# Expert stage of a two-block network: two-part gather and scatter matmuls, six weight slots, interleaved pairs of experts

## The reference

```python
def hier_moe(h, w_rg, b_rg, w_re, b_re, w_eg, w_eu, w_ed):
    ...                                  # router: 2 of 32 experts for each token
    for e in range(N_EXPERTS):           # 32
        hid = jax.nn.silu(t @ w_eg[e]) * (t @ w_eu[e])       # 1024 -> 512
        out = out + gates[:, e:e + 1] * (hid @ w_ed[e])      # 512 -> 1024
    return out.reshape(bsz, s, d)
```

## Time and profile before

| | us |
|---|---|
| median of 3 runs | 2285.81 |
| fastest and slowest run | 2283.96, 2295.26 |
| span of the profiled execution | 2275.8 |

### The profile page before, as it was taken

The page is one execution under the profiler, slowest core; times in us unless marked ns, Lnnn a source line. Parts: engine busy times, 40 slices in busy tenths (PEclk is TensorE's granted clock), DMA queues, the critical chain, the costliest instruction groups (busy, mean ns, idle before and its releaser), DMA issues.

```text
span 2275.8 us, 29449 instructions
## 1 busy us (share of the span) xinstructions
PE 1985.1 (87%) x11980; PEld 1551.8 (68%) x11980; DVE 871.2 (38%) x1464; ACT 735.0 (32%) x1018; POOL 119.3 (5%) x112
## 2 busy tenths in 40 slices
PE   7967798888898777999988879987799998797997
PEld 5844443334443377778887879877787888797986
DVE  3052121111221232533355756533343335575653
ACT  1230011111111132557345434322255634533432
POOL 0000000000000000320210000000031030000000
PEclk9987899999999975999999989998599999998999
DMA  5403588988988732223223334543123322342452
GB/s 208 178 1 157 233 352 337 379 368 360 375 361 359 321 139 107 75 98 126 78 109 148 130 114 180 202 168 141 75 75 111 112 111 101 123 148 112 186 192 102
DMA packets 30887, 412.36 MB, mean 181 GB/s; under 512 B 3600, under 2 KB 5040, under 8 KB 5808
## 3 DMA queue, kind: packets, MB, share of 16 engines
q1 hardware_dynamic: 30768, 410.68, 46.0%
HBM read 408.84 MB, written 1.84 MB: 180 GB/s over the span
## 4 chain that ended last, share of the span: by engine, by line
issue 86%; PE 6%; POOL 5%; DVE 1%; DMA 1%; ACT 0%; SPq 0%; POOLq 0%; DVEq 0%; ACTq 0%
POOL work_mem L1650 5%; PE bank L703 3%; PE bank L711 2%; DMA work_mem<-in_const 1%; PE bank L798 0%; PE bank L735 0%; PE bank L780 0%; POOL small L1658 0%; PE bank L737 0%; PE bank L738 0%; DVE ht_mem L1689 0%; PE bank L773 0%; DVE work_mem L1809 0%; POOL small L1631 0%; DVE work_mem L1826 0%
## 5 line engine op out<-in xcount | busy, mean ns | idle before, releaser
L926 PE MATMUL bank<-wring,gates_mem 128*64 128x512 f32 x1024 | 238.5, 623 | 47.3 <-DMA wring<-in_w 40.7
L2012 DVE TENSOR_TENSOR w_lo<-wring,w_hi 128x2048 fp32r<-128x2048 f32 x88 | 201.3, 2292 | 188.2 <-ACT w_hi L1445 188.2
L1445 ACT ACTIVATE w_hi<-wring 128x2048 fp32r<-128x2048 f32 x88 | 168.5, 1915 | 303.4 <-PE bank L1002 171.8
L1001 PE MATMUL bank<-mixed_hi,w_hi_early 128*128 128x256 f32 x960 | 243.7, 291 | 6.8 <-DVE mixed_lo L2020 4.2
L1445 ACT ACTIVATE w_hi_early<-wring 128x2048 fp32r<-128x2048 f32 x80 | 152.9, 1912 | 265.3 <-PE bank L1002 176.1
L1002 PE MATMUL bank<-mixed_lo,w_hi_early 128*128 128x256 f32 x960 | 238.3, 285 | 0.0
L2012 DVE TENSOR_TENSOR w_lo<-wring,w_hi_early 128x2048 fp32r<-128x2048 f32 x80 | 183.2, 2290 | 124.7 <-ACT w_hi_early L1445 124.7
L926 PEld LDWEIGHTS bank<-wring,gates_mem 128*64 128x64 f32 x1024 | 88.4, 143 | 192.3 <-issue 192.3
L1006 PE MATMUL bank<-mixed_hi,w_lo 128*128 128x256 f32 x1472 | 208.8, 285 | 0.0
L1001 PEld LDWEIGHTS bank<-mixed_hi,w_hi_early 128*128 128x128 f32 x960 | 186.3, 194 | 12.3 <-issue 6.1
L1006 PEld LDWEIGHTS bank<-mixed_hi,w_lo 128*128 128x128 f32 x1472 | 192.2, 194 | 0.0
(11 more groups left out here) (404 smaller groups left out, 3216.2 us busy)
## 6 DMA issues: line engine op xcount, KB each, us to landing
wring<-in_w SPq DMA_DIRECT2D x192, 2048.0 KB, 8.4
cst<-in_const SPq DMA_DIRECT2D x1, 1273.0 KB, 7.6
prm<-in_prm SPq DMA_DIRECT2D x3, 381.0 KB, 8.5
x_mem<-in_x SPq DMA_DIRECT2D x1, 1024.0 KB, 4.9
out_x<-x_mem SPq DMA_DIRECT2D x1, 1024.0 KB, 3.9
rel_skew<-work_mem SPq DMA_DIRECT2D x1, 768.0 KB, 3.5
work_mem<-in_prm SPq DMA_DIRECT2D x1, 512.0 KB, 12.3
work_mem<-rel_skew SPq DMA_DIRECT2D x1, 512.0 KB, 3.6
```

The source lines that it names most:

```text
L926: mm = pe.matmul(out[half, :], x_e[:, pair, k, half], w[e][:, k, :], start=(k == 0), stop=(k == KT - 1))
L1001: pe.matmul(out, w[0][:, k, cols], x[0][:, k, :], start=(k == 0), stop=False)
L1445: act.activation(hi, w, ACT.Copy).then_inc(hi_ready, 1)
L2012: dve.tensor_tensor(lo, w, hi, ALU.subtract).then_inc(lo_ready, 1)
```

## The change

- **Gather.** The normed rows `xn` are split once into `xn_hi` (ACT) and `xn_lo` (DVE), both fp32r. `pick` is done once a turn for both pairs: for each of eight column tiles and two token tiles, `xn_hi` and `xn_lo` are the weights, and all 256 columns of `one_hot` move. Four banks instead of two and two. ACT, not DVE, writes `x_e`, times the gain.
- **Scatter.** `turn` now transposes the bare 0/1 matrix, and two small matmuls give each place its gate weight (`slot_gate`). The output of `down` is scaled by it and split into `ye_hi` (ACT) and `ye_lo` (DVE); `spread` sums both pairs and both parts in PSUM: 16 fp32r matmuls a turn in four banks, and DVE adds to `x` four times a turn, not eight.
- **Order.** pick, both turns, gate 0, up 0, gate 1, flip 0, up 1, down_a 0, flip 1, down_b 0, down_a 1, down_b 1, spread.
- **Slots.** Six: the four of `wring`, `work_mem[:, 0:4096]` and `yt_mem`. The chunks are loaded in the new order of use. The first six are issued in the first block, each as its slot comes free, with semaphores of their own.
- `slots` of the next turn is made after `up 0`.

```diff
-MOE_STEPS = [("pick", 0), ("turn", 0), ("gate", 0), ("up", 0), ("pick", 1), ("flip", 0), ("turn", 1), ("down", 0),
-             ("gate", 1), ("up", 1), ("spread", 0), ("flip", 1), ("down", 1), ("spread", 1)]
-MOE_JOBS = {"pick": 2, "down": 2, "spread": 4}
+MOE_STEPS = [("pick", 0), ("turn", 0), ("turn", 1), ("gate", 0), ("up", 0), ("gate", 1), ("flip", 0), ("up", 1),
+             ("down_a", 0), ("flip", 1), ("down_b", 0), ("down_a", 1), ("down_b", 1),
+             ("spread_a", 0), ("spread_b", 0)]
+MOE_JOBS = {"pick": 4, "spread_a": 2, "spread_b": 2}
+MOE_SLOTS = 6
+MOE_CHUNKS = [(w, pair, e) for w, pair in (("gate", 0), ("up", 0), ("gate", 1), ("up", 1), ("down", 0), ("down", 1))
+              for e in range(2)]
...
-    x_e, hid_b, hid_t = view(gates_mem, 0, PAIRS, KT, P), view(gates_mem, 2048, PAIRS, 512), view(gates_mem, 3072, PAIRS, 4, P)
-    y_b, spread_w = view(gates_mem, 4096, PAIRS, D), view(gates_mem, 6144, PAIRS, S)
-    one_hot, weighted = (view(gates_mem, at, TT, 2 * PAIRS, CAP) for at in (6656, 7168))
+    x_e, hid_b, hid_t = view(gates_mem, 0, KT, PAIRS, P), view(gates_mem, 2048, PAIRS, 512), view(gates_mem, 3072, PAIRS, 4, P)
+    ye_hi = view(parts("ye_hi", "gates_mem", 4096, PAIRS * D), 0, PAIRS, D)
+    ye_lo = view(parts("ye_lo", "ht_mem", 0, PAIRS * D), 0, PAIRS, D)
+    spread_w = view(parts("spread_w", "gates_mem", 6144, PAIRS * S), 0, PAIRS, S)
+    one_hot = view(parts("one_hot", "gates_mem", 6656, 2 * TT * PAIRS * CAP), 0, TT, 2 * PAIRS, CAP)
+    one_hot_f, weighted = (view(gates_mem, at, TT, 2 * PAIRS, CAP) for at in (6656, 7168))
+    xn_hi = view(parts("xn_hi", "work_mem", 4096, TT * D), 0, TT, D)
+    xn_lo = view(parts("xn_lo", "xn_mem", 0, TT * D), 0, TT, D)
...
+            return slot(s)
+        return work_mem[:, 0:CHUNK_COLS] if s == SLOTS else yt_mem
...
+        def expert_chunk(c, turn):
+            sp.dma_start(moe_slot(c), d["w1"][PRE_CHUNKS + chunk_from[c] + turn * turn_chunks]).then_inc(
...
+        for c, j in ((0, pre["kd"][1]), (1, pre["vd"][1]), (4, pre["pv"][1]), (2, pre["out"][1]), (3, pre["out"][3]),
...
             sp.wait_ge(bank_full[j.bank], j.count())
-        sp.wait_ge(rel_loaded, 16)
...
-        for j in pre["ydt"]:
-            sp.wait_ge(bank_read[j.bank], j.count())
-        sp.dma_start(gain_row, d["gain"][0]).then_inc(gain_loaded, 16)
-        with sp.Fori(0, MOE_TURNS) as turn:
-            for c in range(turn_chunks):
-                j = moe[chunk_users[c - SLOTS]][-1]
-                sp.wait_ge(bank_full[j.bank], j.count(turn - 1 if c < SLOTS else turn))
-                sp.dma_start(slot(c), d["w1"][PRE_CHUNKS + c + turn * turn_chunks]).then_inc(w_landed[c % SLOTS], 16)
-        for c in range(turn_chunks - SLOTS, turn_chunks):
+            expert_chunk(c, 0)
+            if c == 4:
+                for j in pre["ydt"]:
+                    sp.wait_ge(bank_read[j.bank], j.count())
+                sp.dma_start(gain_row, d["gain"][0]).then_inc(gain_loaded, 16)
+        with sp.Fori(0, MOE_TURNS - 1) as turn:
+            for c in range(MOE_SLOTS, turn_chunks + MOE_SLOTS):
+                j = moe[chunk_users[c - MOE_SLOTS]][-1]
+                sp.wait_ge(bank_full[j.bank], j.count(turn))
+                if c < turn_chunks:
+                    expert_chunk(c, turn)
+                else:
+                    expert_chunk(c - turn_chunks, turn + 1)
+        for c in range(MOE_SLOTS, turn_chunks):
+            j = moe[chunk_users[c - MOE_SLOTS]][-1]
+            sp.wait_ge(bank_full[j.bank], j.count(MOE_TURNS - 1))
...
-                        for k in range(4):
+                        for k in range(2):
+                            cols = slice((2 * n + k) * P, (2 * n + k + 1) * P)
                             for i in range(TT):
-                                mm = pe.matmul(psum[j.bank][:, k * P:(k + 1) * P], xn[:, i, (4 * n + k) * P:(4 * n + k + 1) * P],
-                                               one_hot[:, i, two, :], start=(i == 0), stop=(i == TT - 1))
-                        if n == 0:
...
+                                pe.matmul(psum[j.bank][:, k * S:(k + 1) * S], xn_hi[:, i, cols], one_hot[:, i],
+                                          start=(i == 0), stop=False)
+                                mm = pe.matmul(psum[j.bank][:, k * S:(k + 1) * S], xn_lo[:, i, cols], one_hot[:, i],
+                                               start=False, stop=(i == TT - 1))
+                        mm.then_inc(r.bank_full[j.bank], 1)
...
-                        mm = pe.transpose(out[:, i * P:(i + 1) * P], weighted[:, i, two, :], ident)
+                        pe.transpose(out[:, i * P:(i + 1) * P], one_hot_f[:, i, two, :], ident)
+                    for i in range(TT):
+                        mm = pe.matmul(out[:, S:S + 1], weighted[:, i, two, :], C("one"), start=(i == 0), stop=(i == TT - 1))
+                    mm.then_inc(r.bank_full[j.bank], 1)
...
+                        if step == "gate" and pair == 0 and k % 2 == 0:
+                            copied(r["pick", 0][k // 2])
...
+                elif step in ("down_a", "down_b"):
+                    n = ("down_a", "down_b").index(step)
+                    if n == 0:
+                        copied(r["flip", pair][0])
+                    w = weights("down", pair)
+                    ready(j)
+                    for ft in range(4):
+                        for e in range(2):
+                            half = slice(e * CAP, (e + 1) * CAP)
+                            mm = pe.matmul(out[half, :], hid_t[:, pair, ft, half], w[e][:, ft, n * 512:(n + 1) * 512],
+                                           start=(ft == 0), stop=(ft == 3))
+                    mm.then_inc(r.bank_full[j.bank], 1)
...
-                            mm.then_inc(r.bank_full[j.bank], 1)
-                mm.then_inc(r.bank_full[j.bank], 1)
...
+                            w = spread_w[:, p, i * P:(i + 1) * P]
+                            pe.matmul(psum[j.bank][:, :], w, ye_hi[:, p, cols], start=(p == 0), stop=False)
+                            mm = pe.matmul(psum[j.bank][:, :], w, ye_lo[:, p, cols], start=False, stop=(p == PAIRS - 1))
+                        mm.then_inc(r.bank_full[j.bank], 1)
+        pe.wait_ge(xn_lo_ready, 1)
...
+            experts(first_pass, turn, turn, 0)
         for j in last_in_bank([j for step in MOE_STEPS for j in moe[step]]):
             pe.wait_ge(bank_read[j.bank], j.count(MOE_TURNS - 1))
...
+        act.wait_ge(xn_ready, 4)
+        act.activation(flat(xn_hi), flat(xn), ACT.Copy).then_inc(xn_hi_ready, 1)
...
+                        for k in range(2):
+                            kt = 2 * n + k
+                            ins = act.activation(x_e[:, kt].rearrange("p a s -> p (a s)"), got[:, k * S:(k + 1) * S], ACT.Copy,
+                                                 scale=at1["norm2"][:, kt:kt + 1])
...
+                        ins = act.activation(slot_gate[:, pair:pair + 1], got[:, S:S + 1], ACT.Copy)
                     elif step == "flip":
...
+                        if half == 0:
+                            used = r["turn", pair][0]
+                            act.wait_ge(r.bank_read[used.bank], used.count(at))
+                        act.activation(ye_hi[:, pair, half * 512:(half + 1) * 512], got[:, :], ACT.Copy,
+                                       scale=slot_gate[:, pair:pair + 1]).then_inc(r.ye_hi_ready, 1)
+                        continue
                     ins.then_inc(r.bank_read[j.bank], 1)
...
+        dve.wait_ge(xn_hi_ready, 1)
+        dve.tensor_tensor(xn_lo, xn, xn_hi, ALU.subtract).then_inc(xn_lo_ready, 1)
...
-                    if step == "pick":
-                        dve.wait_ge(r.bank_full[j.bank], j.count(at))
-                        ins = dve.tensor_tensor(x_e[:, pair, 4 * n:4 * n + 4, :], got[:, :].rearrange("p (k s) -> p k s", k=4),
-                                                gain[:, 4 * n:4 * n + 4, :].to_broadcast([P, 4, P]), ALU.mult)
...
-                            used = r["turn", pair][0]
-                            dve.wait_ge(r.bank_full[used.bank], used.count(at))
-                            dve.wait_ge(r.slots_ready, made + 1)
-                            slots(r, turn + 1, made + 1)
-                        half, i = divmod(n, 2)
-                        xs = x[:, i, half * 512:(half + 1) * 512]
...
+                if (step, pair) == ("up", 0):
+                    used = r["turn", PAIRS - 1][0]
+                    dve.wait_ge(r.bank_full[used.bank], used.count(at))
+                    dve.wait_ge(r.slots_ready, made + 1)
+                    slots(r, turn + 1, made + 1)
```

More of the change, by code:

```diff
@@ L509, in program @@
                          [sem(f"more_bank{b}_read") for b in range(BANKS)],
[L510 removed]
+                         [sem(f"more_weights{s}_landed") for s in range(MOE_SLOTS)])
     SLOTS_MADE = MOE_TURNS + 1
     turn_chunks = PAIRS * PAIR_CHUNKS
[L513 removed]
```

(25 more changed lines are left out.)

94 lines of the change are left out of this document (49 added, 45 removed).

## The result

| | before | changed |
|---|---|---|
| median of 4 runs, us | 2290.53 | 2195.84 |
| lowest and highest, us | 2283.96, 2297.35 | 2188.58, 2197.82 |
| ratio to before | | 0.9586, interval [0.9555, 0.9618] |
| profiled execution: span, us | 2275.8 | 2186.8 |

The kernel got faster by 94.7 us, 4.1%. Among all executions behind this document one stands apart: 4949.4 us, one of six of the four-slot kernel with interleaved steps and five and six added matmuls, and it is left out there. Of the 89.0 us between the two profiled spans, 85.4 lie before the end of the last `down`.

The account below looks back on a forecast made before the run. PE and weight loads, both nearly full in the expert stage, were taken to wait for each other in turn. With loads setting a 59.1 us turn, the stage ends 83.3 us earlier: 2285.8 - 83.3 = 2202.5 us, range 2188 to 2235.

Parts of the forecast that it names:

- The sum: Expert stage: first issue 250.0, plus 12.6 and 433.4, gives 696.0; last down ends at 702.9, stage ends 83.3 us earlier.
- the queue never runs dry: Six slots at the boundary of turns: 5.6 us left against the 2.8 us around an issue, so loads never run out.
- Two bounds on a turn: Expert-stage turn: 54.6 us at most for PE against 59.1 us for the loads, so the loads set it.
- The 9.85 us for a pair of chunks: Expert loads: with loads queued, two chunks, 4.194 MB, take 9.85 us at 426 GB/s; six pairs take 59.1 us.
- Its starting value, 60.8: PE's own turn before the change: 67.55 us less 6.8 us of waits for weights, giving 60.8 us.
- the first issue: SP's first load issue in the expert loop, forecast at 250.0 us of the trace, allowing 248.5 to 253.
- the small matmuls: Gate weights of the places: four tiny float32 matmuls a turn, eight records, 1.2 us more for PE.
- Covers costed at nothing: Copies and splits hidden behind other work; uncovered, gather's last copy adds under 1 us a turn, splitting xn 4 us once.
- 10.0 us to lie around the span: Step from trace to runs: the span of 2275.8 us lies 10.0 below the median, and the difference carries over.
- Loads with gaps: Rival for the expert loads: gaps or a lower rate, 10.49 us a pair, 28 us more, 2231 us; chance 0.17.
- a long-run limit: Rival for the expert loads: bursts paid back, 372 GB/s, 11.27 us a pair, 62 us lost, 2265 us; chance 0.05.
- The clock: Rival for PE's weight steps: clock falls to 1.2 GHz at every step, turn 96 us, time 2498 us; chance 0.03.

## Why the prediction was right, point by point

- **The time.** 2202.5 was forecast, 2195.8 measured, in the range of 2188 to 2235. The sum said that the last `down` ends at 702.9 us of the trace; it ended at 700.8. The mechanism is the one forecast: the queue never runs dry and the loads set the turn, as the two runs with less PE work and with half of the loads show.
- **Two bounds on a turn.** PE at most 54.6 us, loads 59.1. Measured: 51.7 (half loads) and 58.9. The 9.85 us for a pair of chunks, read from one pair of rows, was right to 0.5%. PE's bound was 3 us high. Nearly all of it is the short gaps that I had left in and that went away, 0.82, 0.47, 0.69 and 0.74 us in a turn of the run with six slots alone. Its starting value, 60.8, was near by luck: it is a turn of 67.55 less the stage's mean wait of 6.8, while that turn's own waits are 1.51 + 2.77 + 1.44 = 5.7. That gives 61.8, and 60.5 without its slow step (8.42 for 7.09), as the run with six slots alone then showed (60.53). The error did no harm, as it was not the bound that decided. Nor did the choice of a turn shorter than the mean of 69.7, since the sum goes from the first issue to the last `down` and not by turns.
- **The single terms.** The gather takes 3.8 us a turn, the scatter 3.7 and the small matmuls 0.8 and not 1.2. The first issue came at 247.83 and not 250.0, by small things: the gather began 0.8 us earlier, took 5.9 us and not 6.4, and the small steps behind it took 1.3 us and not 2. The first of these is luck: the router's matmuls took 5.15 us and not 7.01. And the prediction's own terms (234.17, 6.4, 2 and 6.9) add up to 249.5, not to its 249.8.
- **Covers costed at nothing.** Copies of the gather, the split of the output, the split of `xn`: no wait of PE for any of them. The early loads are worth nothing, as said.
- **The size.** The gain measured is 94.7 us and not 83.3. 2.1 us are in the stage and 3.6 behind it, by the profiles; the other 5.7 lie between spans and medians. The median of before rose from 2285.8 to 2290.5 with the fourth run, 14.7 us above its span, while the changed kernel's is 9.0 above its own. The later runs of before, with medians of 2282.4 to 2286.3, make it likely that 2290.5 is high, and the gain nearer to 87 to 90 us. One step of mine was wrong here: I took 10.0 us to lie around the span. It is 1.8 (2188.58 for a span of 2186.8 in the changed kernel); the rest of the 10.0 is that the profiled execution of before was a quick one. That the changed kernel was profiled in a quick execution too, the fastest of its four, is luck, and it made the difference carry over.
- **Loads with gaps, and a long-run limit.** 427 to 428 GB/s held in six turns on end, some 350 us. Both rivals fell for six slots. With them fell, for this case, the rule of the Trainium skill (DMA: Bandwidth & Descriptors, "Where 436 GB/s comes from") that about 358 binds on loads from HBM. Lower rates did come back with four slots, in the windows near the hand-overs (320 to 369 GB/s).
- **The clock.** Waits of 1.8 to 2.8 us went on as before, the turn's PEclk was 0.97 to 1.00, and what slow steps there were lay in the loads' shadow. The mechanism is real, and with four slots and the pairs apart it ate a part of what the shorter PE work could have given: 2.0 of the 5.1 us by which the mean turn of 70.0 exceeds the worked-out 64.9. There a slow step delays the next load, while with six slots it doesn't. The Trainium skill's account (TensorE: Matmul & The Clock Gate, "HAM oscillation — how this bites in real kernels"), a clock that falls in each wait for loads, agrees with the four-slot kernels' rows for their long waits: behind 4.4 to 6.4 us of idle time the steps took 8.4 to 10.1 us. Behind the changed kernel's waits, all under 3 us, some steps were slow (8.78 for 7.09, 5.35 for 3.65) and most were not.
- **The shares.** I had weighed the PE work and the slots as one sum, and so the prediction does not say what each alone brings. Alone, the two-part matmuls bring nothing (2283.5) and the slots 3.0%; on top of the slots the two-part matmuls bring the last 18 us, of which (60.5 - 58.9) x 8 = 13 us are the turns; the rest lies within the spread of the runs.

## What to carry to other kernels

Work out one period for each resource by itself (PE's steps end to end, bytes at the rate of a full queue) and one for the loop of waits (slot freed, issue, landing, user); the longest is the period. With too few slots the loop decides, and then less work on the engine brings nothing: in these runs it only waited more, and behind waits of about 5 us its next step took 9 us and more in place of 7.1. Once the loads set the period, order and PE work are free to be simple.

## What was not expected

- A step behind an idle time of 4.4 to 6.4 us took 8.4 to 10.1 us, and one behind 1.1 to 3.2 us took 8.5 to 8.8 in some turns, in place of 7.09. Filling the wait with matmuls brought it back to 7.09 and in most turns moved the slow step to the next wait.
- The full queue held 427 to 428 GB/s over whole turns, yet where the queue was nearly dry windows of 2 us show 320 to 369 GB/s, so that a pair queued early still landed 1.3 us late.
- ACT's scaled split of the `down` output from PSUM takes 0.69 us, its plain copy of the same size took 0.60; DVE's part takes 0.75. Both hid behind PE.
